# Convolution taps that read their tile in PSUM, with the multiply in place and one wait per bank

## The reference

```python
h = rmsnorm_2(x, norm_mix)
q, k, v, z, xbc, dt_raw, g_lru, x_lru = split_cols(h @ w_in)
att = dilated_attention(q, k, v)
ssd = ssd_mixer(z, xbc, dt_raw, ssd_conv_w, ssd_conv_b, ...)   # silu(conv(xbc)); dt = softplus(dt_raw + bias)
lru = rglru_mixer(g_lru, x_lru, lru_conv_w, lru_conv_b, ...)   # gates from conv(x_lru), then a scan
x = x + concatenate([att, ssd, lru]) @ w_out

def causal_depthwise_conv(x, w, b):
    y = b + xp[:, k_width - 1:] * w[k_width - 1]
    for k in range(k_width - 1):
        y = y + xp[:, k:k + s] * w[k]
    return y                                                   # k_width = 4
```

## Time and profile before

| what | value |
|---|---|
| median of 3 runs | 2056.57 us (2053.7 to 2062.21) |
| profiled execution, its own time | 2057.34 us |
| its span in the profile | 2055.3 us |
| TensorE busy | 1930.0 us, 94% |
| VectorE, ScalarE, GpSimd busy | 41%, 41%, 44% |
| mean granted clock of TensorE | 0.953 |
| the mix stage's part around the change | about 1345 to 1472 us |

### The profile page before, as it was taken

How to read it: one execution, slowest core, us unless ns; L and a number is a source line. 1 busy time by engine, 2 the same in 40 slices (tenths; PEclk the granted TensorE clock), 3 DMA queues, 4 the chain that set the end, 5 groups by cost and what they waited for, 6 DMA issues and landing times.

```text
span 2055.3 us, 26036 instructions
## 1 busy us (share of the span) xinstructions
PE 1930.0 (94%) x9160; PEld 1557.4 (76%) x9160; DVE 841.8 (41%) x1409; ACT 841.3 (41%) x1217; POOL 900.1 (44%) x432
## 2 busy tenths in 40 slices
PE   2878999999999999899999999998999999999997
PEld 1767878888887687557888888875886778888886
DVE  6993232222005589862422220267467233222103
ACT  4455444343214443563543431234435344433221
POOL 6663434444444143393444444333434435444441
PEclk7677999999999799999999999999999999999998
DMA  2003223223322122102323222232320113233231
GB/s 94 23 18 141 100 76 109 100 84 101 102 93 98 52 82 72 52 1 72 99 96 102 96 98 94 90 99 74 132 73 31 62 62 119 86 102 102 92 102 41
DMA packets 51664, 170.70 MB, mean 83 GB/s; under 512 B 6672, under 2 KB 11536, under 8 KB 50960
## 3 DMA queue, kind: packets, MB, share of 16 engines
q1 hardware_dynamic: 50448, 166.59, 24.3%
q10 hardware_dynamic: 1152, 3.26, 0.5%
HBM read 165.37 MB, written 2.10 MB: 81 GB/s over the span
## 4 chain that ended last, share of the span: by engine, by line
PE 74%; DVE 13%; DVEq 4%; POOL 3%; ACT 2%; issue 2%; ACTq 0%; DMA 0%; SPq 0%
PE ps L228 22%; PE ps L230 22%; PE ps L229 22%; POOL pr L1266 3%; DVE convT L2061 2%; PE ps L1420 2%; PE ps L1422 1%; PE ps L1421 1%; DVE score L1667 1%; PE ps L1469 1%; DVE rope_a L1602 1%; DVE h_lo L1066 1%; DVE top L1663 1%; DVEq L616 1%; DVE xT L991 1%
## 5 line engine op out<-in xcount | busy, mean ns | idle before, releaser
L218 POOL TENSOR_TENSOR w_lo<-raw,w_hi 128x1024 fp32r<-128x1024 f32 x296 | 721.7, 2446 | 1028.5 <-ACT w_hi L211 1028.5
L228 PE MATMUL ps<-h_hi,w_hi 128*128 128x512 f32 (+1 forms) x1456 | 573.0, 394 | 8.5 <-DVE h_lo L1066 4.6
L230 PE MATMUL ps<-h_hi,w_lo 128*128 128x512 f32 (+1 forms) x1456 | 569.1, 391 | 0.0
L229 PE MATMUL ps<-h_lo,w_hi 128*128 128x512 f32 (+1 forms) x1456 | 568.9, 391 | 0.0
L211 ACT ACTIVATE w_hi<-raw 128x1024 fp32r<-128x1024 f32 x296 | 311.6, 1057 | 506.0 <-PE ps L230 443.8
L228 PEld LDWEIGHTS ps<-h_hi,w_hi 128*128 128x128 f32 (+1 forms) x1456 | 273.6, 188 | 69.2 <-issue 8.6
L230 PEld LDWEIGHTS ps<-h_hi,w_lo 128*128 128x128 f32 (+1 forms) x1456 | 273.6, 188 | 58.9
L229 PEld LDWEIGHTS ps<-h_lo,w_hi 128*128 128x128 f32 (+1 forms) x1456 | 273.8, 188 | 58.4 <-issue 0.5
L228 PE MATMUL ps<-hid_hi,w_hi 128*128 (+1 forms) x528 | 205.4, 389 | 0.0
L229 PE MATMUL ps<-hid_lo,w_hi 128*128 (+1 forms) x528 | 205.4, 389 | 0.0
L230 PE MATMUL ps<-hid_hi,w_lo 128*128 (+1 forms) x528 | 205.4, 389 | 0.0
(11 more groups left out here) (363 smaller groups left out, 2263.4 us busy)
## 6 DMA issues: line engine op xcount, KB each, us to landing
raw<-in_w_gu SPq DMA_DIRECT2D x132, 512.0 KB, 3.4
raw<-in_w_down SPq DMA_DIRECT2D x66, 512.0 KB, 3.4
raw<-in_w_mix SPq DMA_DIRECT2D x33, 512.0 KB, 3.4
raw<-in_w_dsa SPq DMA_DIRECT2D x29, 512.0 KB, 3.4
raw<-in_w_glu SPq DMA_DIRECT2D x16, 512.0 KB, 3.5
raw<-in_w_out SPq DMA_DIRECT2D x12, 512.0 KB, 3.4
raw<-in_w_o SPq DMA_DIRECT2D x8, 512.0 KB, 3.4
s_x<-in_xs SPq DMA_DIRECT2D x1, 2048.0 KB, 10.1
```

What stands on the lines that cost most here:

```text
L218: pool.tensor_tensor(w_lo[slot][:], raw[slot][:], w_hi[slot][:].bitcast(F32), ALU.subtract)\
L228: pe.matmul(o, wh, ah, start=start, stop=False)
L229: pe.matmul(o, wh, al, start=False, stop=False)
L230: return pe.matmul(o, wl, ah, start=False, stop=stop)
```

## The change

The multiply by the factors writes back into the PSUM bank that it reads. The first tap on ScalarE and the three taps on VectorE read this bank; `t32` is no longer used here. The instructions' number, order and sizes stay. The single wait ahead of the gate rows' projection is taken out, and its first matmul into each of the banks 0 to 3 waits for that bank's convolution instead.

```diff
@@ project
-        def project(pe, w0, group_half, units, in_ready=None, width=GROUP, n_kt=2, nm=None, aside=None, before_unit=2, after_kt=None):
+        def project(pe, w0, group_half, units, in_ready=None, width=GROUP, n_kt=2, nm=None, aside=None, before_unit=2, after_kt=None, banks_free=None):
...
                         o = ps[:, 4 * group_half + tb, 0:width]
+                        if kt == 0 and banks_free is not None:
+                            pe.wait_ge(*banks_free(tb))
                         pe.matmul(o, h_hi[:, kt, toks], wh, start=(kt == 0), stop=False)
@@ mix_tensor
             project_narrow(pe, n_mix + DT0, SH)
-            pe.wait_ge(M["conv_done"], 12 + 4)
...
-            project(pe, n_mix + Z0, 0, 4, aside=running_sums, before_unit=3, after_kt=turn_dt)
+            project(pe, n_mix + Z0, 0, 4, aside=running_sums, before_unit=3, after_kt=turn_dt,
+                    banks_free=lambda tb: (M["conv_done"], 12 + tb + 1))
@@ mix_scalar, tap
-                act.activation(convT[:, index, :].rearrange("p a t -> p (a t)"), t32[b % 2][:], ACT.Identity,
+                act.activation(convT[:, index, :].rearrange("p a t -> p (a t)"), ps[:, b, :], ACT.Identity,
                                bias=w[:, CW:CW + 1], scale=w[:, CW - 1:CW]).then_inc(M["tap_ready"], 1)
@@ mix_vector, taps
-                x = t32[bank % 2]
+                x = ps[:, bank, :]
                 dve.wait_ge(unit_used, done(number))
-                dve.tensor_tensor(x[:], ps[:, bank, :], factors[:], ALU.mult).then_inc(M["scaled"], 1)
+                dve.tensor_tensor(x, x, factors[:], ALU.mult).then_inc(M["scaled"], 1)
```

## The result

The changed kernel takes 2046.45 us, the kernel before beside it 2062.32 (medians of 10 runs each); the ratio is 0.9942, 95% interval 0.9926 to 0.9959. The forecast was 2044.7 us, in a range of 2041.0 to 2050.5, and a gain of 0.58%, which is also what the ratio says. As the interval's upper end is 0.9959, the runs don't settle on which side of 0.5% the gain lies. The ratio is not the quotient of the two medians, which is 0.9923 (15.9 us): each kernel's ten times form two groups (before, 2051.9 to 2056.6 and 2062.2 to 2064.3; changed, 2040.8 to 2044.4 and 2048.5 to 2049.5), and the median of the kernel before lies in its upper group, that of the changed kernel between its two. Group against group the means differ by 11.4 and 14.0 us.

A forecast was written before the change was run, and what follows sets the result against it. TensorE, busy 94%, bounds the kernel, standing 9.0 us for VectorE's late taps. Gains 9.2 + 0.6 + 0.8 + 2.7 less new waits 0.2 and 1.2 give 11.9 us: 2044.7 us, range 2041.0 to 2050.5.

The forecast's parts named there:

- The taps' source: VectorE's middle tap in the loop, reading PSUM, is no longer held by GpSimd's subtraction: 0.75 us instead of 2.70.
- The multiply in place: VectorE's multiply writing PSUM takes 0.70 us against 0.68; ScalarE's 0.81 us may fall a little; nothing counted.
- The new rhythm: VectorE's loop bank takes 4.41 us instead of 6.36, under TensorE's 5.44, leaving 0.9 us slack before the gate projection.
- The waits and the clock: TensorE's gate projection starts 10.6 us earlier (9.2 + 0.6 + 0.8), and 2.7 us of slow clock behind the wait goes.
- The waits bank by bank: At the gate projection, four waits cost nothing; as cover if taps stay held, nine matmuls run ahead, 2.0 us.
- What is late next: Behind the gate projection's start, TensorE newly waits 0.1 to 0.2 us at the running sums and 1.2 at VV0.
- given-back gain: Rival, 1 in 6: a second GpSimd subtraction delays the dt chain 2.3 us; gain 9.6 us, time 2047.0.
- Not freed: Rival, 1 in 11: taps stay held despite PSUM, only nine matmuls run ahead, 2.0 us; time 2054.6 us.
- slower: Rival, 1 in 25: taps from PSUM are long by themselves while TensorE writes other banks; at 1.7 us each, 2070.

The follow-up runs named there:

- short subtractions: Kernel before, taps reading SBUF, GpSimd's subtractions for ten weight units beside the taps cut from 1024 columns to 8; ratio 0.9921.
- half of the banks: Changed kernel with the taps of even banks reading SBUF again, those of odd banks still PSUM; ratio 0.9943.
- filled wait: Kernel before with 39 extra, unused matmuls put between the narrow projection and TensorE's wait for the taps; ratio 0.9979.

## Why the prediction was right

*The taps' source.* Taken: 0.75 us, from the row of L2166; bounds 0.75 and 2.70. Measured: 746 to 753 ns over all 36 in the kernel with the PSUM source alone. The short subtractions show that the hold was GpSimd's, the half of the banks that the second SBUF input decides which tap is held. The Trainium skill ("SBUF — State Buffer", Who interferes with whom) says this in both directions, the free case only for instructions outside VectorE's two-port modes; the taps agree. The 62 more cycles that the Trainium skill ("VectorE: DVE Perf Modes", The TRN2 errata) lists for a PSUM source are not seen: 0.749 us from PSUM, 0.751 from SBUF (medians of the line).

*The multiply in place and ScalarE's tap.* Counted at nothing. The multiply takes 0.691 us against 0.684, ScalarE's tap 0.780 against 0.816; neither is on the path.

*The new rhythm.* 4.38 us for a loop bank, 4.41 predicted. Before, the last bank's third tap was held too, by a second subtraction (2.54 us at 1422.03); the prediction doesn't name it, but its 9.2 us, a gap of starts, hold it. Slack of 0.9 us predicted ahead of the gate projection; the last tap ends at 1418.99 and the first gate matmul starts at 1419.79, 0.8.

*The waits and the clock.* Predicted for the start of the gate projection 10.6 us earlier: from the first multiply it was 71.57 us and is 60.38, 11.2 earlier. That is 0.6 more, in part since TensorE loses more at each small stop than the list of waits shows: from 1394.38 to 1395.57 is 1.19, less 0.227 (the distance between two matmuls' starts) 0.96, where the list says 0.8, and at the other stop 0.79, where it says 0.6. The other 0.3 us were not traced. The slow clock's 2.7 us is 2.4 when it is taken away alone (the filled wait, which still has a stop of 0.3 us in it).

*The waits bank by bank.* Nothing beside a PSUM source, and 2.0 us without it: shown by the two halves run apart (0.0 and 2.1).

*What is late next.* Predicted: 0.1 to 0.2 us at the running sums and 1.2 at VV0; measured 0.4 and 1.0 by the list of waits. dtA was forecast to end 78.0 us after the first multiply (1431.1) and ends after 77.8. That these waits hang on ScalarE's exponentials, which had come to stand behind the end of the narrow projection, is shown by moving them: 1.44 us back. The forecast of VV0, 11.9 us earlier, compares with 12.08.

*The rivals.* The given-back gain didn't come: one subtraction falls on the dt chain as before, no second one. VectorE and GpSimd in the changed kernel:

```profile
1431.80 2.23 DVE L1771 TENSOR_SCALAR dts<-dts 128x32 f32<-128x32 f32 x1
```

```profile
1431.58 2.42 POOL L218 TENSOR_TENSOR w_lo<-raw,w_hi 128x1024 fp32r<-128x1024 f32 x1 [8.01 <-ACT w_hi L211]
```

The prediction spoke of the chain's instructions with both inputs in SBUF. This one has a single SBUF tensor as input and is held all the same, to 1434.03, where the subtraction ends at 1434.00; before, as L1769, it started 0.1 us ahead of the subtraction and took 0.18 us. So two SBUF inputs are not the only form that is held. Not freed and slower are excluded by the taps' durations.

*The total.* Told in starts, the terms are 11.2 us at the gate projection, 2.6 of slow clock (5.42 less 2.81) and 1.7 lost behind it, 12.1 in all, against 10.6 + 2.7 - 1.4 = 11.9; two misses of 0.6 and 0.3 us partly cancel. For the time itself, the forecast of 2044.7 us started from a median of 2056.6, while the ten runs of the kernel before gave 2062.32: 11.9 us less than that would have been 2050.4. That 2046.45 lies so near the forecast is partly luck, and the stretch, 12.08 against 11.9, is the firmer match. The changed kernel's second set of runs gave 2044.56; the executions of the two sets are up to 9 and 5 us apart. Which clock the S5 layer gets in an execution was not in the prediction's terms, and what decides it stays open: no run here aimed at it. Behind VV0 the pair of profiles differs by 2.1 us. Most of it lies in the few us behind one short stop at the norm after the attention (1.5 us in both, L1026). The tables by stretches, before and then changed:

```profile
1690.00:1694.00 4.00, 4.00 (x13) 3.18 (x12) 0.74 (x5) 3.97 (x4) 1.67 (x1) 0.60 0.01 2
```

```profile
1684.27:1688.27 4.00, 4.00 (x20) 3.29 (x19) 0.48 (x3) 3.97 (x4) 2.07 (x1) 1.00 0.01 2
```

The clock of 0.60 is a mean of the two levels over 4 us. Counted from the first large matmul behind the stop (1689.30 and 1683.16), the next twelve start within 4.42 us in one and 2.83 us in the other: 1.6 us that the edit did not earn.

## What to carry to other kernels

When an instruction of VectorE takes several times its usual length, look at what GpSimd does in the same microseconds: here, moving one of two SBUF inputs to PSUM, where the tile lay already, cured it without removing any work, and doing it for every second bank gave nearly all of the gain. An instruction with one SBUF input can be held too (L1771). Price a stop of TensorE by its idle time and by the first microseconds behind it in the timeline. When a chain becomes early, follow the one that waits for it on the other engines: here 1.4 us went to two exponentials that stood behind a wait in ScalarE's list.

## What was not expected of the hardware

Stops of TensorE of 0.8 to 1.0 us left the granted clock at 1.00 (before, at 1395; changed, at 1444), while stops of 7.0 and 9.0 us were both followed by 5.4 to 5.7 us at half of it: shortening the stop by 2 us gave nothing of the slow clock back. And the same stop behind the attention (1.5 us) was followed by a clock of 0.60 in one profile and of 1.00 in another, so a difference of 1.6 us between two profiles can come from there alone.
